# Large weights of a two-layer hybrid block laid out with one contiguous run per partition

## The reference

```
def run_block(args):
    tok, e = args
    xb = h_pad[tok]
    return (jax.nn.silu(xb @ w_gate[e]) * (xb @ w_up[e])) @ w_down[e]
```

## Time and profile before

| | us |
|---|---|
| median of 3 runs | 2122.52 (2120.34 to 2124.36) |
| the profiled execution | 2125.06 |
| its span, first to last instruction | 2121.7 |
| PE busy | 1842.4 (87%) |
| DVE / ACT / GpSimd busy | 790.6 / 575.3 / 84.4 |
| moved by DMA | 361.32 MB, mean 170 GB/s |
| packets | 198588, of them 198176 under 8 KB |
| SP's queue (q1) | 175696 packets, 316.30 MB, 41.8% of 16 engines' span |
| GpSimd's queue (q0), ACT's queue (q10) | 23.99 MB, 18.75 MB |

### The profile page before, as it was taken

One profiled execution on the slowest core, in us unless ns is written; L12 is line 12 of the kernel. 1 busy time (PEld: TensorE's weight loads), 2 busy tenths in 40 slices (PEclk: granted clock), 3 DMA queues, 4 the chain that ended last, 5 costly groups with the idle time before them and its releaser, 6 DMA issues.

```text
span 2121.7 us, 35932 instructions
## 1 busy us (share of the span) xinstructions
PE 1842.4 (87%) x15501; PEld 1123.7 (53%) x15501; DVE 790.6 (37%) x1664; ACT 575.3 (27%) x1198; POOL 84.4 (4%) x74
## 2 busy tenths in 40 slices
PE   5999999899899669999995699999699974999873
PEld 3455668666555345555542355468476433555532
DVE  2433456678711431111103442256688123111003
ACT  2213233467500401111110313223477031111100
POOL 0000000100100000000001000000100000000001
PEclk9999999999999869999997799999899996999986
DMA  9531100480251957799986112001001065999953
GB/s 366 211 116 53 30 26 25 118 260 1 80 198 35 343 176 278 256 329 338 385 312 246 34 33 92 30 1 50 21 1 68 13 216 192 367 386 383 386 227 129
DMA packets 198588, 361.32 MB, mean 170 GB/s; under 512 B 12216, under 2 KB 74176, under 8 KB 198176
## 3 DMA queue, kind: packets, MB, share of 16 engines
q1 hardware_dynamic: 175696, 316.30, 41.8%
q0 software_dynamic: 6736, 23.99, 3.5%
q10 hardware_dynamic: 16000, 18.75, 2.5%
HBM read 318.25 MB, written 40.77 MB: 169 GB/s over the span
## 4 chain that ended last, share of the span: by engine, by line
PE 73%; DVE 11%; DMA 6%; ACT 5%; SPq 3%; issue 2%; POOL 0%; ACTq 0%; DVEq 0%; POOLq 0%
PE ps L1252 14%; PE ps L908 14%; PE ps L1275 7%; PE ps L1175 7%; PE ps L893 5%; PE ps L1018 4%; PE ps L1052 3%; PE ps L877 2%; PE ps L1077 2%; PE ps L857 2%; PE ps L1312 2%; ACT arena L1573 1%; DMA arena<-y_rows,dest 1%; PE ps L1233 1%; SPq L783 1%
## 5 line engine op out<-in xcount | busy, mean ns | idle before, releaser
L1252 PE MATMUL ps<-arena 128*32 128x256 f32 x6080 | 353.9, 386 | 13.0 <-DMA arena<-in_moe_w_up 11.6
L908 PE MATMUL ps<-arena 128*128 128x256 f32 (+2 forms) x1056 | 347.4, 484 | 0.9 <-ACT arena L1447 0.9
L1252 PEld LDWEIGHTS ps<-arena 128*32 128x32 f32 x6080 | 203.2, 112 | 147.0 <-issue 21.5
L908 PEld LDWEIGHTS ps<-arena 128*128 128x128 f32 x1056 | 198.2, 191 | 129.5 <-issue 115.4
L2310 DVE TENSOR_TENSOR arena<-ps,arena 128x128 f32<-128x128 f32 x95 | 27.7, 292 | 496.4 <-ACT arena L1669 496.4
L1275 PE MATMUL ps<-arena 128*32 128x256 f32 x3040 | 183.3, 382 | 1.9 <-DVE arena L2316 1.4
L1175 PE MATMUL ps<-arena 128*128 128x512 f32 (+1 forms) x384 | 138.8, 522 | 2.0 <-DVE arena L2032 2.0
L893 PE MATMUL ps<-arena 128*128 128x256 f32 (+1 forms) x384 | 130.1, 499 | 11.8 <-ACT arena L1421 11.6
L1018 PE MATMUL ps<-arena 32*128 32x256 f32 (+5 forms) x528 | 132.1, 511 | 9.0 <-ACT arena L1573 4.9
L1573 ACT ACTIVATE arena<-ps,att_small 128x768 f32<-128x768 f32 (+2 forms) x160 | 123.2, 773 | 19.2 <-DVE att_small L1951 16.0
L1275 PEld LDWEIGHTS ps<-arena 128*32 128x32 f32 x3040 | 89.8, 109 | 62.6 <-DVE arena L2316 1.7
(11 more groups left out here) (332 smaller groups left out, 2018.4 us busy)
## 6 DMA issues: line engine op xcount, KB each, us to landing
arena<-in_moe_w_gate SPq DMA_DIRECT2D x32, 2048.0 KB, 14.0
arena<-in_moe_w_up SPq DMA_DIRECT2D x32, 2048.0 KB, 20.5
arena<-in_moe_w_down SPq DMA_DIRECT2D x32, 2048.0 KB, 13.9
arena<-in_w_mod SPq DMA_DIRECT2D x24, 2048.0 KB, 17.8
y_rows<-zeros_t SPq DMA_DIRECT2D x2, 9216.0 KB, 52.4
arena<-in_w_in SPq DMA_DIRECT2D x6, 2048.0 KB, 7.8
arena<-in_w_in SPq DMA_DIRECT2D x8, 1024.0 KB, 5.9
y_rows<-arena ACTq DMA_DIRECT2D x76, 96.0 KB, 6.8
```

The source lines that it names most:

```text
L908: last = pe.matmul(PS[:, 4 + k % 2, 0:ch[2]], aT[:, c, t * P:(t + 1) * P], wbuf[:, j % 2, c, 0:ch[2]], start=(c == 0), stop=(c == DC - 1))
L1252: last = pe.matmul(PS[32 * q:32 * q + 32, 2 + g % 2, 0:2 * P], xT(k % 2)[:, a:a + SUB], gate_up_cols(r, c, q), start=(c == 0), stop=(c == ...
```

## The change

Nothing of what is computed or of its order is changed. On the host, before the launch, the large weights are copied into another order, so that what a partition gets from one load is one contiguous run. The loads become flat copies: 16 KB per partition for `w_mod`, gate, up, down and the 512-wide chunks of `w_in`, 13.25 KB and 8 KB for the narrower chunks, 12, 12 and 8 KB for `w_out`. The 424-wide chunk is one load in place of two, and the semaphore counts of `win_in` follow. A chunk of `w_in` narrower than 512 lies with its own width as row step in the buffer, where the buffer had a step of 512 before; PE's operands address it so. Bytes, buffers and waits are as they were.

```
+        WIN_W = [ch[2] * P if ch[0] == "x" else ch[2] for ch in CH]
+        WIN_AT = [sum(WIN_W[:q]) for q in range(len(CH) + 1)]
+        def wflat(j):
+            return ar(A_E + (j % 2) * (E_W // 2), DC * WIN_W[j])
+        def wchunk(j):
+            return wflat(j).rearrange("p (k n) -> p k n", k=DC)
...
-            n = [sum(1 if CH[q][0] == "x" else len(CH[q][3]) for q in range(top) if q % 2 == j % 2) for top in (NCH, j + 1)]
+            n = [sum(1 for q in range(top) if q % 2 == j % 2) for top in (NCH, j + 1)]
...
-                sp.dma_start(mod_w(i).rearrange("p (k n) -> p k n", k=DC),
-                             io["w_mod"][L].rearrange("(k p) n -> p k n", p=P)[:, :, n * 512:(n + 1) * 512]
-                             ).then_inc(S(f"wmod_in{i % 5}"), 16)
+                sp.dma_start(mod_w(i), io["w_mod"][L, n]).then_inc(S(f"wmod_in{i % 5}"), 16)
...
-                        for o, a, w in ch[3]:
-                            sp.dma_start(b[:, :, o:o + w], src[:, :, a:a + w]).then_inc(S(f"win_in{j % 2}"), 16)
+                sp.dma_start(wflat(j), io["w_in"][L][:, DC * WIN_AT[j]:DC * WIN_AT[j + 1]]).then_inc(S(f"win_in{j % 2}"), 16)
...
-                    sp.dma_start(ar(wo_at[c0], (c1 - c0) * D).rearrange("p (k n) -> p k n", k=c1 - c0), wov[:, c0:c1, :]
+                    sp.dma_start(ar(wo_at[c0], (c1 - c0) * D), io["w_out"][L][:, c0 * D:c1 * D]
...
-                    for dst, v in ((gate_w(pos), wgv), (up_w(pos), wuv)):
-                        sp.dma_start(dst, v[bass.ds(e, 1)].rearrange("e p k n -> p (e k) n")).then_inc(S(f"gu_in{pos % 3}"), 16)
+                    for dst, v in ((gate_flat(pos), wgv), (up_flat(pos), wuv)):
+                        sp.dma_start(dst, v[bass.ds(e, 1)].rearrange("e p n -> p (e n)")).then_inc(S(f"gu_in{pos % 3}"), 16)
...
-                    sp.dma_start(down_w(pos), wdv[bass.ds(e, 1)].rearrange("e p k n -> p (e k) n")
+                    sp.dma_start(down_flat(pos), wdv[bass.ds(e, 1)].rearrange("e p n -> p (e n)")
...
-                                                     wbuf[:, j % 2, c, mm * P:(mm + 1) * P], aT[:, c, a:b],
+                                                     wchunk(j)[:, c, mm * P:(mm + 1) * P], aT[:, c, a:b],
...
-                                             wbuf[:, j % 2, c, 0:ch[2]], start=(c == 0), stop=(c == DC - 1))
+                                             wchunk(j)[:, c, :], start=(c == 0), stop=(c == DC - 1))
...
+    for nm, kc in (("moe_w_gate", DC), ("moe_w_up", DC), ("moe_w_down", FC)):
+        data[nm] = _np.ascontiguousarray(data[nm].reshape(LAYERS, EXP, kc, P, -1).transpose(0, 1, 3, 2, 4)).reshape(LAYERS, EXP, P, -1)
+    data["w_mod"] = _np.ascontiguousarray(data["w_mod"].reshape(LAYERS, DC, P, 12, 512).transpose(0, 3, 2, 1, 4)).reshape(LAYERS, 12, P, -1)
+    data["w_out"] = _np.ascontiguousarray(data["w_out"].reshape(LAYERS, DC, P, D).transpose(0, 2, 1, 3)).reshape(LAYERS, P, -1)
```

More of the change, by code:

```diff
@@ L240, in build @@
         sq2 = ar(A_RAW, 2 * N).rearrange("p (b n) -> p b n", b=2)
-        wbuf = ar(A_E, E_W).rearrange("p (b k n) -> p b k n", b=2, k=DC)
         kTm = ar(A_F, 4 * N).rearrange("p (h n) -> p h n", h=4)
@@ L610, in ysb, with gate_flat, up_flat, down_flat @@
             return ar(M_Y + par * D, D)
+        def gate_flat(pos):
+            return ar(M_GU[pos % 3], DC * FF)
+        def up_flat(pos):
+            return ar(M_GU[pos % 3] + DC * FF, DC * FF)
+        def down_flat(pos):
+            return ar(M_D[pos % 2], FC * D)
         def gate_w(pos):
-            return ar(M_GU[pos % 3], DC * FF).rearrange("p (k n) -> p k n", k=DC)
+            return gate_flat(pos).rearrange("p (k n) -> p k n", k=DC)
         def up_w(pos):
-            return ar(M_GU[pos % 3] + DC * FF, DC * FF).rearrange("p (k n) -> p k n", k=DC)
+            return up_flat(pos).rearrange("p (k n) -> p k n", k=DC)
         def down_w(pos):
-            return ar(M_D[pos % 2], FC * D).rearrange("p (k n) -> p k n", k=FC)
+            return down_flat(pos).rearrange("p (k n) -> p k n", k=FC)
         def gate_up_cols(pos, c, q):
@@ L750, in _ @@
                 sp.wait_ge(S("var_f"), L + 1)
-                wov = io["w_out"][L].rearrange("(k p) n -> p k n", p=P)
                 for c0, c1 in ((0, 3), (3, 6), (6, 8)):
-                    sp.dma_start(ar(wo_at[c0], (c1 - c0) * D).rearrange("p (k n) -> p k n", k=c1 - c0), wov[:, c0:c1, :]
+                    sp.dma_start(ar(wo_at[c0], (c1 - c0) * D), io["w_out"][L][:, c0 * D:c1 * D]
                                  ).then_inc(S("wo_in"), 16)
@@ L765, in _ @@
                                  ).then_inc(S("wr_in"), 16)
-                wgv = io["moe_w_gate"][L].rearrange("e (k p) n -> e p k n", p=P)
-                wuv = io["moe_w_up"][L].rearrange("e (k p) n -> e p k n", p=P)
-                wdv = io["moe_w_down"][L].rearrange("e (k p) n -> e p k n", p=P)
+                wgv, wuv, wdv = io["moe_w_gate"][L], io["moe_w_up"][L], io["moe_w_down"][L]
                 def expert_at(pos):
@@ L820, in _ @@
                     sp.wait_ge(S("t_pe"), 4 * o + (2 * L + 1))
-                    for dst, v in ((gate_w(EXP - 1), wgv), (up_w(EXP - 1), wuv)):
-                        sp.dma_start(dst, v[bass.ds(e, 1)].rearrange("e p k n -> p (e k) n")).then_inc(S("t_gu"), 16)
+                    for dst, v in ((gate_flat(EXP - 1), wgv), (up_flat(EXP - 1), wuv)):
+                        sp.dma_start(dst, v[bass.ds(e, 1)].rearrange("e p n -> p (e n)")).then_inc(S("t_gu"), 16)
                     sp.wait_ge(S("t_pe"), 4 * o + (2 * L + 2))
-                    sp.dma_start(down_w(EXP - 1), wdv[bass.ds(e, 1)].rearrange("e p k n -> p (e k) n")).then_inc(S("t_wd"), 16)
+                    sp.dma_start(down_flat(EXP - 1), wdv[bass.ds(e, 1)].rearrange("e p n -> p (e n)")).then_inc(S("t_wd"), 16)
             for i in range(NT - CT):
@@ L2463 @@
     data = {k: _np.ascontiguousarray(inputs[k]) for k in _INS}
+    for nm, kc in (("moe_w_gate", DC), ("moe_w_up", DC), ("moe_w_down", FC)):
+        data[nm] = _np.ascontiguousarray(data[nm].reshape(LAYERS, EXP, kc, P, -1).transpose(0, 1, 3, 2, 4)).reshape(LAYERS, EXP, P, -1)
+    data["w_mod"] = _np.ascontiguousarray(data["w_mod"].reshape(LAYERS, DC, P, 12, 512).transpose(0, 3, 2, 1, 4)).reshape(LAYERS, 12, P, -1)
+    data["w_out"] = _np.ascontiguousarray(data["w_out"].reshape(LAYERS, DC, P, D).transpose(0, 2, 1, 3)).reshape(LAYERS, P, -1)
+    w4 = data["w_in"].reshape(LAYERS, DC, P, N_IN).transpose(0, 2, 1, 3)
+    parts = [[(XBC0, 4 * P)], [(XBC0 + 4 * P, 2 * P)], [(MLA0, 416), (DT0, 8)], [(NA0 + 256, 512)], [(DIF0 + 256, 512)], [(NA0, 256)], [(DIF0, 256)], [(Z0, 256)]]
+    data["w_in"] = _np.concatenate([_np.concatenate([w4[:, :, :, a:a + w] for a, w in part], axis=3).reshape(LAYERS, P, -1) for part in parts], axis=2)
     data["near"] = _np.ascontiguousarray(rel[:, :, near_index()].transpose(0, 3, 1, 2, 4)).reshape(LAYERS, P, -1)
```

## The result

The changed kernel takes 2144.75 us in the median (2142.33 to 2147.12, four runs), the kernel before 2123.44 on the same chip: ratio 1.0101, 95% interval 1.0082 to 1.0120. It is slower by 21.3 us, 1.0%; the spans of the profiled executions are 2121.7 and 2144.3 us.

What follows compares the result with a forecast made beforehand. PE was taken as the bound nearly everywhere; -17.5 - 4.2 - 1.3 + 26.9 = +3.9 us on a median of 2122.52 gave 2126.5 us. The range was 2101 to 2146, the forecast's own 2118 to 2136.

Steps and rivals of the forecast that it cites:

- rival B: Turns as in part 3, and delayed stores also tear the expert loops: 2138 us, up to 2148; chance 0.14.
- part 3: Small transfers beside 16 KB packets wait 0.55 us per turn, one packet of each queue in turn: +26.9 us.
- Part 1: Layer 1's experts: weights at 426 GB/s instead of 387, all listed PE stalls go: -17.5 us.
- the cover of the stores in the loops: Expert loops: a 96-row item's stores take 22 us, buffer wanted after 23; 0 to 6 us if torn, taken as 0.
- Part 2: Routing: stores of routed rows wait less behind six expert loads; -4.2 us in layer 0, -1.3 in layer 1.
- Layer 0's store: Before layer 0's extra block: 28 turns beside long packets delay the last y_rows store, 9.98 us before, by +10.5 us.
- its combine gather: Layer 0's combine: first pair of gathers, 8.54 us before, has 18 packets per engine beside w_mod and w_in: +8.4 us.
- layer 1's block gather: Layer 1's extra block: nine turns for the gather that took 8.59 us: +3 us (0 to +4).
- The two first gathers: First gather of each layer's experts: some five of seven turns beside gate loads, +2.5 us each, +5.0 together.
- Part 4: Load issue on SP: SP held less by full queues, order and waits unchanged: 0 us (0 to -1).
- A: Turns not by whole 16 KB runs, so part 3 falls away: 2099.5 us, or 2105 at a lower rate; chance 0.25.
- C: No gain in rate, 387 GB/s stays: 2149.5 us with the turns, 2122.5 without; chance 0.03.

Runs made afterwards that it cites:

- experiment 5: Changed kernel with four y buffers instead of two in layer 1's expert loop: 2141.1 us, 1.0092 of the kernel before.
- experiment 7: Changed kernel, experts in 4 KB runs, w_mod 2 KB, w_in and w_out whole: 2115.5 us; then experts in 8 KB, four y buffers: 2115.8 us.

## Why the prediction was right or wrong

The time lies in the range, near its slow end, only because the range reached out to rival B; the forecast's own 2118 to 2136 missed, and its likeliest value, 2126.5, was 18 us short. What happened is rival B in kind, to which I gave 0.14: the turns as in part 3, the stores' delay that also tears layer 1's loop, and weights that come too slowly. That the number was inside was in part luck.

**Part 1, the rate: right; the stage: wrong.** Alone, 16 KB runs give 432 GB/s, where I took 426. The stage gained 6.8 us, not 17.5. Two steps failed. The larger is DMA's work per expert, "14.8 + 1.2 (stores, 0.39 MB) + 1.0 (gather, 0.39 MB) = 17.0, so no backlog grows any more". DMA view of 1850 to 1937.5 us, five items' periods, changed kernel:
```profile
DMA packets 4739, 34.18 MB, mean 391 GB/s; under 512 B 609, under 2 KB 2405, under 8 KB 2885
...
q1 hardware_dynamic: 2067, 30.16, 86.3%
q0 software_dynamic: 560, 1.97, 7.3%
q10 hardware_dynamic: 2099, 1.84, 6.5%
```
At 391 GB/s an item's 7.08 MB take 18.1 us, and PE's period is 17.4. In their 86.3% of the engines' time the weights moved at 399 GB/s, not 426 (15.8 us an item for 14.8), and the gather took 1.3 us for 1.0. So a backlog did grow, more slowly than before. The down loads, issued every 17.4 us from 1835 us on, landed after 10.7, 11.1, 12.1, 13.7, 13.9, 14.6, 14.8 and 16.0 us; the same eight before, from 1812 us on, after 9.6 to 19.8 us.

The smaller is the cover of the stores in the loops, "28 x 0.6 + 5 = 22 us", wanted after 23. I compared one item's latency with its cover, but every item stores: the next four stores stand in the same queue 17.4 us later. The view above has one packet to one, as the earlier trace rows had shown for short stretches. An item needs some 28 turns per engine. At 0.6 us and its own packet's few hundredths that is 18 us against a period of 17.4, so the backlog grows from item to item: 2099 packets are 131 per engine, 4.7 items' worth in five periods. ScalarE's timeline in the changed kernel (its copy into the y buffer, and in brackets the wait before it):
```profile
1858.63 0.38 ACT L1680 ACTIVATE arena<-ps 128x256 f32<-128x256 f32 x1 [1.97 <-DMA y_rows<-arena]
...
1877.53 0.38 ACT L1680 ACTIVATE arena<-ps 128x256 f32<-128x256 f32 x1 [3.92 <-DMA y_rows<-arena]
...
1896.33 0.38 ACT L1680 ACTIVATE arena<-ps 128x256 f32<-128x256 f32 x1 [5.33 <-DMA y_rows<-arena]
...
1916.15 0.38 ACT L1680 ACTIVATE arena<-ps 128x256 f32<-128x256 f32 x1 [7.76 <-DMA y_rows<-arena]
...
1952.63 0.39 ACT L1680 ACTIVATE arena<-ps 128x256 f32<-128x256 f32 x1 [9.46 <-DMA y_rows<-arena]
...
1972.32 0.38 ACT L1680 ACTIVATE arena<-ps 128x256 f32<-128x256 f32 x1 [11.75 <-DMA y_rows<-arena]
```
Until 1973 us this costs PE nothing; then the wait is longer than ScalarE's slack, and PE loses 0.3 to 2.3 us five times (6.0 in all). It is a cliff between 8 KB (10.9 us per store, no such wait in the loop) and 16 KB.

How the missing 10.7 us are made up is shown only in part. The buffer is 2.3 of them (experiment 5): rival B's "+6 in layer 1" matches PE's 6.0 us of waits for DVE. With the buffer free these are gone, but the waits for up rise from 4.4 to 5.7 us, and the two groups of 64 matmuls behind them take 5.2 and 5.4 us in place of 3.7. Without gathers all 10.6 come back, so the rest hangs on the load that small transfers put on a nearly saturated DMA, up to the end of the stage, where 64-row experts want weights every 12 us. There the rate with everything in it rose by 4% and not by 10. DMA view of the kernel before, 1960 to 2020 us, and of the changed one, 1975 to 2035:
```profile
DMA packets 10117, 23.26 MB, mean 388 GB/s; under 512 B 395, under 2 KB 1297, under 8 KB 10109
```
```profile
DMA packets 3314, 24.25 MB, mean 404 GB/s; under 512 B 463, under 2 KB 1771, under 8 KB 1963
```
Of these SP's queue moved 21.69 and 21.99 MB, so most of the gain went to small transfers that were behind. What a gather and a store do to the rate of long packets was not measured by itself and stays open. A part of the 6.8 us is also no gain: since the first gather landed later, PE began later behind a stream of weights that had started on time. From the first store of the routed rows to the extra block's gather the changed kernel gains only 0.7 us (289.2 to 288.5), 4 KB runs 4.8 (284.4), 8 KB runs some 6 (283.2).

**Part 2, routing: too large.** The 3.9 and 2.9 us took all six expert loads at the 2 KB rate; with the down loads at their own 418 GB/s they are 3.2 and 2.2. Layer 0 gained 1.6 us of the 4.2 (the other 1.5 of the -3.1 stood already at 591 us), layer 1 nothing where I had -1.3: the stores landed in 5.99 and 8.30 us.

**Part 3, turns: right in kind, in size right twice and short twice.** Layer 0's store 20.02 us (forecast 20), its combine gather 16.47 (17), layer 1's block gather +2.65 (3). The two first gathers cost 5.1 and 4.9 us, not 2.5 each. From issue to landing the trace has 131 and 168 packets of SP's queue beside them, 8 and 10 per engine where I had counted five turns, and they took 0.77 and 0.73 us each, not 0.615. Per engine that is 6.3 and 7.7 us of weight packets, before 1.3 and 2.7: the whole difference. The sum of this part is 30.6 us against my 26.9.

**Part 4, SP: right.** Of the 45.60 us of the earlier trace rows 31.8 lie between the end of the third load's issue and the fourth's, which has waits for semaphores in front of it; the same four span 55.88 us in the changed kernel. The three loads ahead of it took 13.45 us before (from 1083.46 us on) and now:
```profile
1085.41 2.78 SPq L687 DMA_DIRECT2D arena<-in_w_mod  x3
```
SP is held 10.7 us less here, and nothing came of it, as no load was waiting for SP.

**What is left** is 2.7 us in layer 1's extra block: its 32 and 16 matmuls took 16.94 and 8.72 us where they took 15.83 and 7.13. Over that block the granted clock was 0.84 in the mean (2067 to 2098 us), before 0.92 (2047 to 2075); 1 is the level of 2.4 GHz, so a longer part of it ran at 1.2. The kernels with 4 KB runs have 0.84 there as well, the one with 16 KB experts 0.92, so it doesn't follow the run length; in these and the two kernels compared, PE came out of an experts' stage in which it was 95 to 96% busy. Why the clock falls here in one kernel and not in another stays open. The parts add up to -1.5 - 1.6 + 30.6 - 6.8 + 2.7 = +23.4 us; the spans differ by 22.6.

**Rivals.** A is refuted: a 16 KB run is one packet and one turn. C is refuted by 387, 410, 424 and 432 GB/s at 2, 4, 8 and 16 KB. B I gave 0.14, and its reason, the thin cover, stood in my own numbers (22 against 23). With the period of 17.4 us beside the 18 us of turns it would have been the likeliest case.

The Trainium skill ("DMA: Bandwidth & Descriptors", Specifications) has 512 B as the least transfer for line rate. By these four rates this kernel's trace doesn't agree. The three bus cycles per packet that the Trainium skill charges (same page, Why small descriptors are slow) would give about 4% from 2 to 16 KB, an estimate; measured are 12%.

## What to carry to other kernels

A longer run buys rate for its own queue and is paid by every small transfer on the others, one whole packet per turn: from 2 to 4 KB the rate rose 6% and a turn by 0.06 us, from 4 to 16 KB the rate rose 5% and a turn by 0.4 us. So weigh the length by what runs beside a load, or hold the long load back until the small one is through. Here one length for all, 4 KB, did as well as lengths chosen by neighbour (experiment 7). And for transfers that recur, compare the work of an item with the period of an item, for the bytes of all queues (18.1 against 17.4 us) as for the turns of the small ones (18 against 17.4), not one landing with one cover. Above the period it is a backlog, and further buffers help only until it has filled them.

## Not expected of the hardware

- The price of a long packet depends on what is still ahead of it in its queue: the 16 KB w_mod loads cost the store issued with them nothing behind a down load of 2 KB runs, and 8.7 us behind one of 16 KB runs (20.02 against 11.34 us with w_mod in 2 KB runs).
- 16 KB runs give 432 GB/s alone, but 404 for all queues together with 7% of the engines' time going to 1 KB stores and 4% to gathers (1975 to 2035 us), 6% less; 2 KB runs give 387 alone and 375 with the same 2.1 MB of small transfers (2 KB kernel, 1950 to 2010 us), 3% less. At these two lengths the longer run lost more to the small packets between.
- SP's issue of three w_mod loads at the end of layer 0 took 13.5 us with 2 KB runs and 2.8 us with 16 KB runs.
